# A top-4-of-32 expert block on one core: transposes by VectorE in 32x32 blocks instead of by TensorE

## What is computed

```python
u2 = rms_norm(h, norm_ffn_g)                       # 512 rows of 1024 reach the output
logits = u2 @ router_w + router_b                  # 32 experts
top_val, top_idx = lax.top_k(logits, 4); gates = softmax(top_val)
# for each expert e, over the tokens that chose it:
hcat = x @ w1[e] + b1[e]                           # 1024 -> 2048
h_glu, h_lin = split(hcat); h_glu = minimum(h_glu, 7); h_lin = clip(h_lin, -7, 7)
act = h_glu * sigmoid(1.702 * h_glu) * (h_lin + 1)
y = act @ w2[e] + b2[e]                            # 1024 -> 1024
h = h + sum over the 4 experts of gate * y
```

## Time and profile before

| | |
|---|---|
| time, median of 3 runs | 1778.22 us (1778.15 to 1778.97) |
| span of the profiled execution | 1778.4 us |
| granted TensorE clock in the expert loop | 1.00 of 2.4 GHz |
| one expert, start to start (L1601: 990.41, 1023.59, 1056.77 us) | 33.18 us |
| expert loop, first hidden product to last y_out | 673.48 to 1738.2 us |

### The profile page before, as it was taken

The page is one execution under the profiler, slowest core; times in us unless marked ns, Lnnn a source line. Parts: engine busy times, 40 slices in busy tenths (PEclk is TensorE's granted clock), DMA queues, the critical chain, the costliest instruction groups (busy, mean ns, idle before and its releaser), DMA issues.

```text
span 1778.4 us, 38974 instructions
## 1 busy us (share of the span) xinstructions
PE 1637.7 (92%) x16302; PEld 946.0 (53%) x16302; DVE 640.2 (36%) x1103; ACT 433.3 (24%) x704; POOL 498.4 (28%) x465
## 2 busy tenths in 40 slices
PE   5988798999899938999999999999999999999990
PEld 5988796777687933344344344344344344344340
DVE  3799999411425141131131131131131121221225
ACT  5322212434512142121121121121121121121121
POOL 5555645336143451112112112112111111111112
PEclk9989898999899958999999999999999999999996
DMA  5121312232027426999999999999999999999955
GB/s 172 48 83 59 94 49 71 72 95 86 10 72 283 188 74 249 404 402 382 403 403 381 400 402 382 402 401 381 398 402 378 404 401 383 404 398 386 405 213 240
DMA packets 131256, 482.86 MB, mean 272 GB/s; under 512 B 17013, under 2 KB 58141, under 8 KB 97716
## 3 DMA queue, kind: packets, MB, share of 16 engines
q1 hardware_dynamic: 122084, 464.98, 67.9%
q0 software_dynamic: 8992, 16.85, 2.9%
q10 hardware_dynamic: 144, 0.52, 0.1%
HBM read 474.61 MB, written 16.86 MB: 276 GB/s over the span
## 4 chain that ended last, share of the span: by engine, by line
PE 79%; DVE 8%; issue 7%; DMA 2%; POOL 1%; ACT 1%; DVEq 1%; SPq 0%; POOLq 0%; ACTq 0%
PE banks L1246 37%; PE banks L1302 19%; PE banks L920 17%; DVE conv L1390 3%; PE banks L1290 2%; DVE odd_taps L1390 2%; PE banks L1229 1%; DVE h_res L1631 1%; DVE conv L1381 1%; POOL slot_table L594 1%; PE banks L1097 1%; PE banks L1266 1%; PE banks L1218 1%; DMA x_sb<-in_x_dram 1%; DMA y_in<-y_rows 0%
## 5 line engine op out<-in xcount | busy, mean ns | idle before, releaser
L1246 PE MATMUL banks<-w_ring,xT 128*32 128x512 f32 x6144 | 673.2, 594 | 1.1 <-ACT xT L864 1.1
L1246 PEld LDWEIGHTS banks<-w_ring,xT 128*32 128x32 f32 x6144 | 197.5, 110 | 434.9 <-issue 426.3
L1302 PE MATMUL banks<-w_ring,actT 128*32 128x256 f32 x6144 | 344.8, 380 | 0.0
L535 POOL TENSOR_TENSOR w_lo<-stage,w_hi 128x2048 fp32r<-128x2048 f32 x40 | 248.4, 6211 | 271.4 <-ACT w_hi L670 271.4
L1302 PEld LDWEIGHTS banks<-w_ring,actT 128*32 128x32 f32 x6144 | 193.4, 110 | 129.6 <-issue 5.4
L1601 DVE TENSOR_TENSOR hid<-banks,bias 128x512 f32<-128x512 f32 x96 | 66.4, 692 | 523.4 <-PE banks L1246 523.4
L920 PE MATMUL banks<-u_hi,w_hi 128*128 128x264 f32 (+1 forms) x544 | 187.1, 344 | 23.3 <-DVE conv_in L1402 16.2
L920 PE MATMUL banks<-u_hi,w_lo 128*128 128x264 f32 (+1 forms) x544 | 185.1, 340 | 0.0
L920 PE MATMUL banks<-u_lo,w_hi 128*128 128x264 f32 (+1 forms) x544 | 184.5, 339 | 0.0
L604 POOL COPY token_now<-token_of 96x1 int32 (+1 forms) x34 | 12.6, 372 | 499.5 <-PE banks L1229 495.9
L1624 DVE TENSOR_TENSOR y_out<-banks,bias 128x256 f32<-128x256 f32 x96 | 40.8, 425 | 296.4 <-PE banks L1302 296.4
(11 more groups left out here) (243 smaller groups left out, 1724.7 us busy)
## 6 DMA issues: line engine op xcount, KB each, us to landing
w_ring<-in_expert_w_dram SPq DMA_DIRECT2D x384, 1024.0 KB, 10.0
stage<-in_w_in_dram SPq DMA_DIRECT2D x28, 1024.0 KB, 5.2
y_in<-y_rows SPq DMA_DIRECT2D x3, 2048.0 KB, 12.3
stage<-in_conv_pw_w_dram SPq DMA_DIRECT2D x4, 1024.0 KB, 5.1
stage<-in_mlstm_out_w_dram SPq DMA_DIRECT2D x4, 1024.0 KB, 5.2
stage<-in_w_out_dram SPq DMA_DIRECT2D x4, 1024.0 KB, 6.2
x_sb<-in_x_dram SPq DMA_DIRECT2D x4, 512.0 KB, 7.0
h_res<-in_x_dram SPq DMA_DIRECT2D x1, 2048.0 KB, 11.1
```

The lines of the kernel that those rows point to most:

```text
L535: nc.gpsimd.tensor_tensor(w_lo[:, s], stage[:, s], w_hi[:, s].bitcast(F32), ALU.subtract).then_inc(w_lo_made[s], 1)
L1246: last = nc.tensor.matmul(banks[32 * g:32 * (g + 1), t].rearrange("p (h n) -> p h n", h=2), xT[:, k, 32 * t:32 * (t + 1)], w1_ring[k][:, : ...
L1302: last = nc.tensor.matmul(banks[32 * g:32 * (g + 1), 3 + t, 0:GRP], actT[:, k, 32 * t:32 * (t + 1)], w2_ring[k // 2][:, k % 2, GRP * g:GRP ...
```

## The change

- **Gather.** The token row is fetched in four pieces of 256 floats. `xs` is now 128 partitions x 768: partition 32 g + i holds piece g of slot i, for the three groups t side by side. Three indirect DMAs of 128 x 256 take the place of one of 96 x 1024. The table `piece_of`, computed from `row_of` after all 12 reads of the slot table, takes the place of `token_of`.
- **Transposes.** VectorE's 32x32 block transpose turns `xs` into `xT` (one instruction, 128 x 768) and each `act_v[:, t]` into `actT[:, t]` (128 x 256). The eight transposes of `xs`, the six of the activations on TensorE, and the copies by ScalarE are gone.
- **Order of columns.** A block transpose leaves the 32x32 blocks where they are, so the contraction order is permuted instead: `u2` is written in strips (columns 32 (4 b + g) + j go to 256 g + 32 b + j; four DVE operations of 256 columns in place of one of 1024), the router weights are loaded in the same order by 8 DMAs, and w1 and its bias are streamed as 16 runs of 32 columns, 128 columns apart, in place of two runs of 256.
- **Banks and waits.** The bias product goes to PSUM banks 6 and 7 and no longer waits for `y_made`; second(0) waits for it instead. The second product follows the first with nothing between.

```diff
-        xs = in_stage("xs", [SLOTS, D])
-        xT = in_stage("xT", [P, KT, SLOTS])
+        xs = in_stage("xs", [P, TG * GRP])
+        xT = in_stage("xT", [P, TG, KT, 32])
...
-            sp.dma_start(token_of[:, 0:PASSES * NE].rearrange("i (q e) -> i q e", e=NE), by_slot).then_inc(table_in, 16)
-            for g in range(CG):
-                for t in range(TG):
+            for t in range(TG):
+                for g in range(CG):
                     sp.dma_start(row_of[32 * g:32 * (g + 1), t, 0:PASSES * NE].rearrange("i (q e) -> i q e", e=NE),
                                  by_slot[32 * t:32 * (t + 1)]).then_inc(rows_in, 16)
...
-                pool.indirect_dma_start(out=xs, out_offset=None, in_=u2_dram,
-                                        in_offset=bass.IndirectOffsetOnAxis(ap=token_now, axis=0),
-                                        bounds_check=last_token, oob_is_err=False).then_inc(xs_in, 16)
+                for t in range(TG):
+                    pool.indirect_dma_start(out=xs[:, GRP * t:GRP * (t + 1)], out_offset=None, in_=u2_dram,
+                                            in_offset=bass.IndirectOffsetOnAxis(ap=piece_now[:, t:t + 1], axis=0),
+                                            bounds_check=last_piece, oob_is_err=False).then_inc(xs_in, 16)
...
-                            last = nc.tensor.matmul(banks[32 * g:32 * (g + 1), t].rearrange("p (h n) -> p h n", h=2),
-                                                    xT[:, k, 32 * t:32 * (t + 1)], w1_ring[k][:, :, GRP * g:GRP * (g + 1)],
-                                                    start=k == 0, stop=k == KT - 1, tile_position=(0, 32 * g))
+                            units = w1_ring[k].rearrange("p h (b g j) -> p g (h b) j", g=CG, j=32)[:, g]
+                            last = nc.tensor.matmul(banks[32 * g:32 * (g + 1), t].rearrange("p (c j) -> p c j", j=32),
+                                                    xT[:, t, k], units, start=k == 0, stop=k == KT - 1, tile_position=(0, 32 * g))
...
-                    transposes(0)
-                    transposes(1)
-                    x_transposes(n + 1)
-                    second(0)
-                    transposes(2)
-                    second(1)
-                    second(2)
+                    for t in range(TG):
+                        second(t)
...
-                nc.vector.scalar_tensor_tensor(out=u2[:, i % 2], in0=h_res[:, i], scalar=h_rstd[:, i:i + 1], in1=gf_bc,
-                                               op0=ALU.mult, op1=ALU.mult).then_inc(u2_made, 1)
+                for g in range(CG):
+                    strips = [a.rearrange("p (b g j) -> p g b j", g=CG, j=32)[:, g] for a in (h_res[:, i], gf_bc)]
+                    nc.vector.scalar_tensor_tensor(out=u2[:, i % 2, GRP * g:GRP * (g + 1)].rearrange("p (b j) -> p b j", j=32),
+                                                   in0=strips[0], scalar=h_rstd[:, i:i + 1], in1=strips[1],
+                                                   op0=ALU.mult, op1=ALU.mult).then_inc(u2_made, 1)
...
-            dve.wait_ge(table_in, 16)
-            nc.vector.tensor_scalar(token_of, token_of, 2, None, ALU.arith_shift_right).then_inc(tables_made, 1)
             dve.wait_ge(rows_in, 16 * CG * TG)
+            pieces = piece_of[:, :, 0:PASSES * NE]
+            chain(nc.vector.tensor_scalar(pieces, row_of[:, :, 0:PASSES * NE], 2, None, ALU.arith_shift_right))
+            nc.vector.tensor_scalar(pieces, pieces, float(CG), group_of, ALU.mult, ALU.add).then_inc(tables_made, 1)
             nc.vector.tensor_scalar(row_of, row_of, float(CG), group_of, ALU.mult, ALU.add).then_inc(tables_made, 1)
+            def turn_rows(n):
+                dve.wait_ge(xs_in, (n + 1) * (16 * TG))
+                nc.vector.transpose(xT.rearrange("p t k s -> p (t k s)"), xs).then_inc(xT_made, 1)
+            turn_rows(0)
...
-                        nc.vector.tensor_tensor(act_v[:, t], lin, sig[:, t], ALU.mult).then_inc(act_made, 1)
+                        own(nc.vector.tensor_tensor(act_v[:, t], lin, sig[:, t], ALU.mult))
+                        nc.vector.transpose(actT[:, t].rearrange("p k s -> p (k s)"), act_v[:, t]).then_inc(actT_made, 1)
...
                         activated(t)
                     assert k[0] == STEPS
+                    turn_rows(n + 1)
                     dve.wait_ge(bias_made, n * 3 + 3)
```

More of the change, by code:

```diff
@@ L1223, in _ @@
             places(TT)
[L1225 to L1231 removed]
             pe.wait_ge(wo_out, 2 * TT)
[L1234 removed]
+            pe.wait_ge(logits_mm, TT)
+            pe.wait_ge(mask_made, TT)
             pe.wait_ge(bias_split, PARTS + 3)
@@ L1281, in _ @@
                         last.then_inc(hid_mm, 1)
-                    def transposes(t):
-                        pe.wait_ge(act_made, n * TG + (t + 1))
-                        if t >= 2:
-                            pe.wait_ge(actT_made, n * TG + (t - 1))
-                        for h in range(2):
-                            last = nc.tensor.transpose(banks[:, 6 + t % 2, P * h:P * (h + 1)], act_v[:, t, P * h:P * (h + 1)], ident)
-                        last.then_inc(act_mm, 1)
                     def second(t):
-                        pe.wait_ge(bias_made, n * 3 + 3)
+                        if t == 0:
+                            pe.wait_ge(y_made, n * TG + 1)
                         pe.wait_ge(actT_made, n * TG + (t + 1))
```

100 lines of the change are left out of this document (40 added, 60 removed).

## The result

The change makes the kernel slower: 1800.78 us, median of 4 (1799.09 to 1804.26), against 1778.6 us; ratio 1.0122, 95% interval [1.0106, 1.0138]. I had forecast 1726 us, in a range of 1718 to 1762 us.

A forecast was written before the change was run, and what follows sets the result against it. TensorE was taken to bound the expert loop, with DMA close behind: 1778.4 us less 61 us in the loop plus 8.7 us at the start gave 1726 us, with an 8-in-10 range of 1718 to 1762 us.

The forecast's parts named there:

- The step that failed: GpSimd's issues per expert: three at 1.26 us each, first scatter some 2 us later, costing nothing except behind the last expert.
- TensorE, 1.9 us per expert: Expert loop: gaps of 1.36 us before second(0) and 0.55 us before second(1) go; period 31.3 us, 61 us over the loop.
- VectorE's transposes: Block transposes in the loop: 0.4 us for 256 columns, 0.9 us for 768, hidden by covers, so no price there.
- Weights in runs of 32: Hidden product: TensorE streams w1 in runs of 32 floats at the unchanged pace, 0.43 us for four loads.
- The gather and DMA work, 31.3 us: Per expert: new gather behaves like the scatter, the slow stretch goes, DMA work 31.3 us; with the present gather's disturbance 32.2 us.
- The start, 8.7 us: Before the loop: first hidden product later by 7.5 us for table and gathers plus 1.2 us for u2 (5 to 12).
- the gather's 4.6 us from issue to transpose: Before the loop: time from gather issue to transposes, taken from today's 666.27 to 670.87 us, placing the transpose at 680.0 us.
- The four operations on u2: Before the loop: 425 ns each, 1.70 us against 1.28 us per tile, partly hidden, so 1.2 us (0 to 1.7).
- the slower case: Whole kernel slower than before, through costly gather pieces or TensorE streaming runs of 32 more slowly; chance 0.11.
- each piece costs an engine what a row costs: Rival on gather transfers: 256 pieces per expert take 3.5 us, DMA work 33.9 us, kernel 1793 us; within the slower 0.11.

The follow-up runs named there:

- the versions with six and with sixteen added starts: Version with three gathers in a row in the hidden product, plus six late starts (1739.35 us) or thirteen following directly (1759.03 us), the added ones moving no row.
- the 1827 us version: Changed kernel with six starts of 32-column pieces that move no row added in each expert's hidden product: 1827.26 us.
- one file: Three gathers in a row in the hidden product, thirteen starts moving no row added behind them; run unedited in two batches: 1759.03 and 2135.37 us.

## Why the prediction was wrong

**The step that failed** is "POOL issues three DMAs in place of one ... so this costs nothing except behind the last expert". Each issue took 1.00 to 1.06 us with 0.30 us between, near the price of 1.26 us. But I costed them only by who waits for GpSimd, and put their effect on TensorE at nothing without a row. In the second product three starts and the scatter stand in a row, and the run holds TensorE, which waits for none of them, 2.25 us per expert: 72 us over the loop. Against the span of 1802.2 us the sum closes: 1726.1 + 72.3 for the hold-up + 3.4 behind the last y_out + 2.3 that the loop saved less than 61 - 1.9 for the start. The last two terms cancel, by luck. The version that moves the gathers out of there measured 1730 us, in a batch whose other runs show the hold-up. What happens inside the chip between GpSimd's starts and TensorE stays open; the step that failed does not. In the earlier trace rows a gather and a scatter, 3.5 us apart, were all I had looked at, and no row of before has two starts close together beside the second product.

**TensorE, 1.9 us per expert:** right. Without the hold-up the period is 31.29 us, forecast 31.3, and 58.7 us go between the first hidden product and the last y_out of the profiled executions (1005.6 against 1064.3 us), forecast 61.

**VectorE's transposes:** right. 445 ns for 256 columns and 936 ns for 768 (forecast 0.4 and 0.9), hidden behind the second product. In the loop no wait of TensorE for actT or xT is listed.

```profile
1039.41 0.45 DVE L1584 STREAM_TRANSPOSE actT<-act_v 128x256 f32<-128x256 f32 x1
```

**Weights in runs of 32:** right. Four loads every 0.43 us in the hidden product, as in the earlier trace rows, and 592 ns for one matmul in both kernels.

**The gather and DMA work, 31.3 us:** right as far as it can be read. At a period of 31.29 us the DMA engines are full at 415 GB/s, the stretch at 326 GB/s of the earlier trace rows has no counterpart, and hardly a chunk is waited for. They are at their limit: in the versions with six and with sixteen added starts the loop begins to wait for chunks (5.0 and 15.2 us in all, from 750 to 1700 us, in the second product).

```profile
L1274 PE MATMUL banks<-w_ring,actT 128*32 128x256 f32 x5760 | 320.4, 379 | 5.0 <-DMA w_ring<-in_expert_w_dram 5.0
```

**The start, 8.7 us:** too high; 6.8 us in the profiled execution. From the last start of the slot table's DMAs (662.30 us; 660.91 us in the earlier trace rows) to the first hidden product it is 17.9 us against 12.6: 5.4 us more, where I had 7.5. It is 17.8 us when the changed kernel is profiled again. The term that was mis-sized is the gather's 4.6 us from issue to transpose. I took it from one gather of 96 x 1024; behind the third small one it is 2.7 us:

```profile
676.39 1.01 POOL L610 DMA_INDIRECT xs<-u_rows,piece_now  x1 [0.31 <-issue]
679.13 0.98 DVE L1553 STREAM_TRANSPOSE xT<-xs 128x768 f32<-128x768 f32 x1 [5.99 <-DMA xs<-u_rows,piece_now]
```

The four operations on u2 take 480 ns each, not 425. From the first of them to the first start of the slot table it is 18.9 and 18.2 us in the two profiled executions against 17.4 us: 0.8 to 1.5 us, forecast 1.2.

**The rivals and chances:** the slower case had 0.11, and neither of its mechanisms came. The condition I had named for it ("each piece costs an engine what a row costs") speaks of transfers, and gathers that land nothing cost as much as the real ones. That the time came out above the old one, as these rivals would have it, is no merit of theirs. I had no rival in which the issuing engine disturbs one that doesn't wait for it.

## What to carry to other kernels

When an edit turns one indirect DMA of GpSimd into several, look at which of them now stand in a row and beside what, and try them in another place: here the same three cost 72 us in the product that issues a matmul every 54 ns and nothing in the one with a matmul every 107 ns, or in pairs. In this case a gap "behind issue" on TensorE, together with a reader that waits for "remote" long after the matmul's due time, was the sign that semaphores and matmuls are held back and not that work is missing. And when an experiment comes out free of an effect that others show, repeat it beside the original on one chip before looking for the reason in its edit.

## What the runs showed of the hardware

- A run of indirect DMA starts on GpSimd (1.3 us each) slowed TensorE to about 0.3 of its pace: 5.1 loads per us against 18.5 in the second product, and 11 in 3.98 us, 2.8 per us, against 9.3 in the hidden product. The slowing begins some 2.8 us after the first start in the former (1044.24 to 1047.09 us) and 7.7 us in the latter, that is after some 50 and 70 matmuls, and ends with the run. Three starts in the hidden product last 4 us, less than that, and did nothing; the six in the hidden product of the 1827 us version last 7.8 us, and in about half of the experts the loads of that product show one step of 0.5 to 1.0 us (0.42 us or less is usual), some 8 us after the first start. Between a reserve of instructions and something else that lasts as many matmuls the runs do not decide.
- Whether this happens is not fixed by the program: 1759.03 and 2135.37 us for one file. The changed kernel took 1799 to 1807 us in all eight executions, in two batches, and both profiled ones show the hold-up. What it would take in the other condition was not measured.
- DMA moves 415 GB/s over a whole expert with one core at work. Starts whose indexes are out of bounds still read and take a share: with thirteen of them per expert 480.96 MB are read from memory, against 474.14 MB without them. The 6.8 MB are 416 starts x 128 pieces x 128 bytes. With them GpSimd's queue holds 4.8% of the engines' time against 4.3% with the gathers and scatters alone, and the core moves 402 GB/s against 415 (1000 to 1060 us).
- In the earlier trace rows GpSimd's start takes 0.96 us; beside a VectorE operation (TENSOR_TENSOR) on 3072 columns with two inputs in SBUF (3.35 us, L1542) one such start took 3.67 us in both kernels, and ended 0.8 us after that operation. The Trainium skill, SBUF — State Buffer, section Who interferes with whom, has such an operation contend, through a read port that the two engines share, with a GpSimd instruction that reads SBUF; the 3.67 us agree if the start reads its indexes that way, which no run here shows. In a probe that the section reports, this kind of operation did not stall a DMA; here the start beside it took 3.67 us, and the measurement decides. The same section says that "PE and ACT never wait on anyone" at SBUF. No run here shows TensorE waiting for a port, but it was held back by GpSimd's work in another way that these rows measure, so the sentence is no cover for TensorE.
